# A two-block fp32 transformer on one core: score tiles multiplied apart, tiles moved between engines, SBUF offsets changed

## Chip, cores, metric

The kernel runs on 1 core of one Trainium2 chip. The metric is the time of one execution in device microseconds. The median over several runs counts.

## The reference

Two blocks over 512 tokens of width 1024, all in float32. What the change touches is this (cut):

```python
def gla_chunked(q, k, v, log_f):          # per head: 128 keys, 128 values, chunks of 16 tokens
    ...
    b = jnp.cumsum(log_f, axis=2)
    ...
    q_dec = q * jnp.exp(b)
    k_dec = k * jnp.exp(-b)
    ...

def second_block(x, mem, ...):
    for layer in range(2):
        u = rmsnorm(h, norm_g[layer, 0])
        y = mixer_window_attn(...) if layer == 0 else mixer_hgrn2(...)   # both with cross attention to mem
        h = h + rmsnorm(y, norm_g[layer, 1])
        f = conv_ffn(rmsnorm(h, norm_g[layer, 2]), ...)
        h = h + rmsnorm(f, norm_g[layer, 3])
```

The first block is chunked attention plus a gated convolution and a square-ReLU network of width 4096. The second block has two layers: windowed attention with cross attention, then a gated linear recurrence in both directions (8 heads) with cross attention, each followed by a network of width 2816.

## The kernel before

**Data.** Activations lie feature-major: 8 tiles of 128 features by 512 tokens. Each weight matrix is cut into 128x128 tiles, eight to a slot. SyncE loads 384 slots of 512 KB in a fixed order into a ring of 6 (`w_raw`). GpSimd rounds each slot to a high part `w_hi` and subtracts for a low part `w_lo` (lines 513 to 517; for 40 slots of the recurrence layer ScalarE rounds instead, line 1469). Activations are split the same way. Each weight tile then costs a *triple* on TensorE, three 512-column products on fp32r (`three_passes`, lines 556 to 558): high by high, low activation by high weight, high activation by low weight. The first name in a row such as `acc<-h_hi,w_hi` is the operand that streams, the second the one that is loaded into the array.

**Stages.** `STAGES` (line 61) lists them in the order in which TensorE runs them: six projections of q, k and v, `conv`, `gate`, `proj`, `out`, `up0`, `down0`, `up1`, `down1`, then `a_in`, `memkv`, `a_out`, `ffn_in0`, `ffn_out0`, `b_in`, `b_out`, `ffn_in1`, `ffn_out1`. A stage has column blocks, each of `kt` weight tiles, that add up in one bank of PSUM. A stage in `LEAD` runs its first four column blocks side by side, feature tile by feature tile. `WIDE` (line 59) names stages whose next blocks use banks that are otherwise the attention's (4 and 5 are `ps_s`, 6 is `ps_o`), so that these blocks need not wait until VectorE has taken block 0 (`bank_free`, line 562). `a_out` is not in it.

**Order.** Each engine's instructions are written out by hand in one block per engine, with semaphores between them. There are three attentions. The tiles of projections are interleaved with an attention's units by the table `also`: one unit is scores, maximum, exponential (ScalarE), normalisation (VectorE), transposes (TensorE, `turn`), copy of the transposes to SBUF (ScalarE, `take`, line 1205) and the product with the values (`weigh`, line 727). In the second attention the leading blocks of `a_out` run feature tile by feature tile as soon as each is there (`out_lead`, line 948). The last feature tile is there when ScalarE has copied the last head and VectorE has split it.

**Third attention and recurrence.** While the third attention runs (16 units, from about 1655 to 1696 us), ScalarE also does the first recurrence head's activations: `head_gates(0)` (Silu) after unit 5, `head_sigmoids(0)` after unit 9, `head_forget(0)` after unit 10, `head_logs(0)` after unit 12 (line 1480). Exponential, Silu, Sigmoid and Ln each want a function table of their own. Then come the heads, h = 0 to 7. VectorE keeps the masked scores of a head in `hg_s_f` and `hg_s_b`, computes the states between blocks (`head_states`, line 2061), and adds the two score tiles into `hg_ke_f` (line 2075). TensorE's `head_out` (line 1063) multiplies that sum, and the states, with the values: 4 + 3 + 3 products of 128 columns in full fp32. Each stands as two rows, "x20" for a head. Head h's `head_out` stands in the order of head h+1.

**End.** After the last products VectorE scales each of 8 output tiles and adds it to the residual (`add_norm`, lines 1594 and 1605); SyncE stores them in four pieces of two tiles.

**SBUF.** All offsets are written out (lines 200 to 300). The first tensor starts at byte 16512 of each partition, which is 128 past a multiple of 512. `w_lo`, `w_hi`, `x_res`, `h_hi` and `h_lo` have that same remainder. After the constants come 27 small tensors in steps of 32 bytes, and then a shared part: `rope`, `ffn_tmp`, `rstd_in` and the arena of 96 KB, which holds `qk`, `o_hi`, `o_lo`, `y_hi`, `u_hi`, `u_lo`, `x0_hi`, `hid_hi`, `hid_lo` and the rest by stages. It starts at byte 124608, which is 192 past a multiple of 512 (64 past a multiple of 128). The tensors named here lie multiples of 2048 further on. In `up0` and `up1` feature tile 0 comes from the arena (`x_hi`, `x_lo`) and tiles 1 to 7 from `h_hi` and `h_lo`.

## Time and profile before

| what | value |
|---|---|
| median of 3 runs | 2439.69 us (2438.66 to 2440.32) |
| the profiled execution, own time | 2437.65 us |
| its span, first to last instruction | 2435.9 us |
| TensorE busy | 98% of the span |
| GpSimd, VectorE, ScalarE busy | 60%, 51%, 27% |
| mean granted TensorE clock | 0.993 |

Busy time of TensorE counts each matmul from its start to its end, and these overlap. Its speed is better read from the distance between the starts of two rows. The clock stands at two levels. A share of 1.00 in a window is the full 2.4 GHz, and 0.5 is 1.2 GHz. A number in square brackets behind a row of the timeline is the engine's idle time before it, with the instruction that ended it.

### The profile page before, as it was taken

Reading aid. Unit: us, or ns where it says so; the run is one execution under the profiler, and the core shown is the slowest. Engines: PE = TensorE matmul, PEld = TensorE weight load, DVE = VectorE, ACT = ScalarE, POOL = GpSimd, SP = SyncE. Lnnn points to the kernel's source line nnn. Section 1 sums busy time; section 2 is a strip of 40 time slices with the busy share of each in tenths; the row PEclk is TensorE's granted clock in tenths of the full one; section 3 lists DMA queues with packets and bytes.
Section 4 is the critical chain, followed back from the end, with each engine's and each line's share of the span. In section 5 each row is a group of like instructions: output and inputs, shape, how many; then the busy total and the mean of one; then the engine's idle time right before and its main releaser. Section 6 shows DMA issues by size and latency. Waiting matters only on the chain.

```text
span 2435.9 us, 32669 instructions
## 1 busy us (share of the span) xinstructions
PE 2378.2 (98%) x12126; PEld 1961.1 (81%) x12126; DVE 1231.5 (51%) x2000; ACT 659.7 (27%) x1331; POOL 1466.4 (60%) x1461
## 2 busy tenths in 40 slices
PE   8999999999999999999999999999999999999997
PEld 6877778887888888787788888887888877888885
DVE  4335654334302315777348553044888885755402
ACT  3233321002201213455221110025567643111100
POOL 8654546667666677654458777662344455877761
PEclk9999999999999999999999999999999999999998
DMA  4222222222232322221122222221222212222221
GB/s 169 93 96 87 79 78 97 99 98 88 96 98 98 124 95 87 78 79 62 61 87 96 96 95 95 95 87 53 70 70 70 71 60 78 96 95 97 101 97 52
DMA packets 59762, 214.49 MB, mean 88 GB/s; under 512 B 6624, under 2 KB 6752, under 8 KB 59488
## 3 DMA queue, kind: packets, MB, share of 16 engines
q1 hardware_dynamic: 56880, 206.55, 25.1%
q10 hardware_dynamic: 2736, 5.96, 0.7%
q8 instruction: 97, 1.59, 0.3%
q14 instruction: 49, 0.40, 0.1%
HBM read 210.38 MB, written 2.10 MB: 87 GB/s over the span
## 4 chain that ended last, share of the span: by engine, by line
PE 92%; DVE 5%; ACT 2%; issue 1%; DMA 0%; POOL 0%; DVEq 0%; ACTq 0%; POOLq 0%
PE acc L556 25%; PE acc L558 25%; PE acc L557 24%; PE ps_o L727 2%; PE ps_s L699 2%; PE ps_t L713 2%; PE acc L768 1%; PE acc L770 1%; PE acc L769 1%; PE ps_s L1016 1%; DVE ps_s L1594 1%; PE ps_o L1075 0%; PE ps_s L770 0%; PE ps_s L768 0%; PE ps_s L769 0%
## 5 line engine op out<-in xcount | busy, mean ns | idle before, releaser
L513 POOL CAST w_hi<-w_raw 128x512 fp32r<-128x512 f32 x688 | 439.5, 667 | 709.8 <-DMA w_raw<-stream 709.8
L556 PE MATMUL acc<-h_hi,w_hi 128*128 128x512 f32 (+1 forms) x1844 | 726.0, 394 | 5.5 <-DVE h_lo L1560 2.6
L558 PE MATMUL acc<-h_hi,w_lo 128*128 128x512 f32 (+1 forms) x1844 | 706.7, 383 | 0.0
L557 PE MATMUL acc<-h_lo,w_hi 128*128 128x512 f32 (+1 forms) x1844 | 705.4, 383 | 0.0
L515 POOL TENSOR_TENSOR w_lo<-w_raw,w_hi 128x512 fp32r<-128x512 f32 x384 | 521.6, 1358 | 213.3 <-ACT w_hi L1469 213.3
L517 POOL TENSOR_TENSOR w_lo<-w_raw,w_hi 128x512 fp32r<-128x512 f32 x384 | 534.4, 1392 | 0.0
L556 PEld LDWEIGHTS acc<-h_hi,w_hi 128*128 128x128 f32 x1844 | 348.1, 189 | 73.6 <-DVE h_lo L1560 4.4
L558 PEld LDWEIGHTS acc<-h_hi,w_lo 128*128 128x128 f32 x1844 | 347.2, 188 | 69.8
L557 PEld LDWEIGHTS acc<-h_lo,w_hi 128*128 128x128 f32 x1844 | 348.0, 189 | 65.4 <-issue 1.9
L1616 DVE COPY y_all<-acc 128x512 f32<-128x512 f32 x31 | 21.4, 692 | 269.9 <-PE acc L558 238.5
L556 PE MATMUL acc<-hid_hi,w_hi 128*128 128x512 f32 x352 | 138.9, 395 | 0.0
L558 PE MATMUL acc<-hid_hi,w_lo 128*128 128x512 f32 x352 | 138.0, 392 | 0.0
L557 PE MATMUL acc<-hid_lo,w_hi 128*128 128x512 f32 x352 | 136.6, 388 | 0.0
L1205 ACT ACTIVATE probs_t<-ps_t 128x256 f32<-128x256 f32 (+3 forms) x160 | 68.2, 426 | 240.6 <-PE ps_t L713 240.0
L1638 DVE TENSOR_TENSOR hid_tmp<-acc,rstd_in 128x512 f32<-128x512 f32 x82 | 56.8, 692 | 133.2 <-PE acc L558 130.8
L556 PE MATMUL acc<-u_hi,w_hi 128*128 128x512 f32 x256 | 100.9, 394 | 0.0
L558 PE MATMUL acc<-u_hi,w_lo 128*128 128x512 f32 x256 | 100.4, 392 | 0.0
L557 PE MATMUL acc<-u_lo,w_hi 128*128 128x512 f32 x256 | 99.4, 388 | 0.0
L557 PE MATMUL acc<-o_lo,w_hi 128*128 128x512 f32 x244 | 95.4, 391 | 0.0
L1188 ACT ACTIVATE probs<-probs,neg_max 128x256 f32<-128x256 f32 (+3 forms) x160 | 87.3, 546 | 22.6 <-DVE neg_max L1673 22.4
L1333 ACT ACTIVATE ffn_tmp<-ffn_tmp 128x512 f32<-128x512 f32 x44 | 27.9, 634 | 237.9 <-DVE ffn_tmp L1914 237.9
L1896 DVE TENSOR_TENSOR x_res<-acc,x_res 128x512 f32<-128x512 f32 x16 | 11.1, 692 | 142.8 <-PE acc L558 142.8
(344 smaller groups left out, 3691.0 us busy)
## 6 DMA issues: line engine op xcount, KB each, us to landing
w_raw<-stream SPq DMA_DIRECT2D x384, 512.0 KB, 3.2
toeplitz<-ext_in ACTq DMA_DIRECT2D x16, 256.0 KB, 3.7
out<-x_res SPq DMA_DIRECT2D x4, 512.0 KB, 2.6
x_res<-x_in SPq DMA_DIRECT2D x3, 512.0 KB, 6.8
mem<-mem_in ACTq DMA_DIRECT2D x1, 1024.0 KB, 7.7
consts<-consts_in SPq DMA_DIRECT2D x1, 656.0 KB, 9.3
x_res<-x_in SPq DMA_DIRECT2D x2, 256.0 KB, 5.0
rope<-rope_in ACTq DMA_DIRECT2D x1, 512.0 KB, 9.2
```

Source lines behind the costliest of these rows:

```text
L513: nc.gpsimd.tensor_copy(hi[:, half], raw[:, half]).then_inc(hi_made, 1)
L515: nc.gpsimd.tensor_tensor(lo[:, 0:D // 2], raw[:, 0:D // 2], f32(hi[:, 0:D // 2]), ALU.subtract).then_inc(low_half, 1)
L517: nc.gpsimd.tensor_tensor(lo[:, D // 2:], raw[:, D // 2:], f32(hi[:, D // 2:]), ALU.subtract).then_inc(split_made, 1)
L556: nc.tensor.matmul(ps, hi, x_hi[:, k, 0:cols], start=(k == 0), stop=False)
L557: nc.tensor.matmul(ps, hi, x_lo[:, k, 0:cols], start=False, stop=False)
L558: mm = nc.tensor.matmul(ps, lo, x_hi[:, k, 0:cols], start=False, stop=(k == st.kt - 1))
L699: mm = nc.tensor.matmul(ps_s[i][:, cols], u.q, u.k[:, cols], start=True, stop=True)
L713: mm = nc.tensor.transpose(ps_t[:, b * P:(b + 1) * P], src[:, b * P:(b + 1) * P], const("ident"))
L727: mm = nc.tensor.matmul(ps_o[u.out_part:u.out_part + rows, u.out_cols[0]:u.out_cols[1]], u.v[b], p_t[:, (u0 + 2 * j + i) % 2, b * P:(b + 1 ...
L1188: nc.scalar.activation(p[:, b, 0:u.width], p[:, b, 0:u.width], ACT.Exp, scale=-1.0, bias=small["neg_max"][:, b:b + 1], accum_out=small["ro ...
L1205: nc.scalar.activation(p_t[:, b, 0:u.width], ps_t[:, 0:u.width], ACT.Copy).then_inc(pt_ready, 1)
L1638: step(nc.vector.tensor_tensor(dst, src, by, ALU.mult), st.free)
```

## The change

- `a_out` gets a fifth bank in `WIDE`. Column block 4 uses `ps_s` 0, and its first four tiles run ahead of the last `out_lead`.
- In the third attention ScalarE does the sigmoids, `head_forget(0)` and the logarithms after units 11, 12 and 14, and `head_gates(0)` after the attention.
- VectorE's sum of the two score tiles goes. `head_out` multiplies `hg_s_f` and `hg_s_b` apart, and `hg_chain` is raised by the last state.
- At the end GpSimd handles output tiles 5 and 6: times the gain, times the scale, plus the residual. For that TensorE spreads the scale a second time into `ps_t`, and ScalarE copies it to `rstd_in`. VectorE handles tiles 0 to 4 and 7. The stores are cut 2, 2, 1, 2, 1.
- Six one-column tensors share one place of 32 bytes, and the shared part starts at a multiple of 512 from the first tensor. It now lies at byte 124544, again 128 past a multiple of 512. No other tensor of those named above moves.

```diff
--- before.py
+++ after.py
@@ -56,7 +56,7 @@
 
 
 TOKENS = ["q0", "q1", "k0", "k1", "v0", "v1"]
-WIDE = {"ffn_in0": (4, 5, 6), "ffn_in1": (4, 5, 6), "b_in": (6, 5), "b_out": (4,)}
+WIDE = {"ffn_in0": (4, 5, 6), "ffn_in1": (4, 5, 6), "a_out": (4,), "b_in": (6, 5), "b_out": (4,)}
 LEAD = {*TOKENS, "up0", "memkv", "a_in", "a_out", "ffn_in0", "b_in", "b_out", "ffn_in1"}
 STAGES = [
     *[(name, BANKS, 8) for name in TOKENS], ("conv", 24, 8), ("gate", 16, 8), ("proj", 16, 8), ("out", 8, 8),
@@ -211,15 +211,16 @@
         params = sb("params", [PARAM_W], at)
         at += -(-4 * PARAM_W // 32) * 32
         small = {}
-        for name, n in [("zero", 1), ("k_g8", 1), ("half_gate_b", 16), ("lower", 16), ("one_less", 16), ("less_one", 16), ("eps_d", 1), ("eps_q", 1),
-                        ("eps_v", 1), ("neg_sink", 16), ("neg_max", P_BUFS), ("row_sum", P_BUFS), ("sink_exp", P_BUFS), ("inv_sum", P_BUFS),
+        for name, n in [("half_gate_b", 16), ("lower", 16), ("one_less", 16), ("less_one", 16), ("neg_sink", 16), ("neg_max", P_BUFS), ("row_sum", P_BUFS), ("sink_exp", P_BUFS), ("inv_sum", P_BUFS),
                         ("rms_tok", BLOCKS), ("rstd_tok", BLOCKS), ("eps_tok", BLOCKS),
                         ("head_sums", 16), ("head_root", 16), ("head_inv", 16), ("decay_f", CHUNKS), ("decay_b", CHUNKS),
                         ("block_f", BLOCKS), ("block_b", BLOCKS),
-                        ("lb_exp", 32), ("root_warm", 1), ("rstd_mem", MEM)]:
+                        ("lb_exp", 32), ("columns", 6), ("rstd_mem", MEM)]:
             small[name] = sb(name, [n], at)
             at += -(-4 * n // 32) * 32
-        at = (at + 63) // 64 * 64
+        for i, name in enumerate(["zero", "k_g8", "eps_d", "eps_q", "eps_v", "root_warm"]):
+            small[name] = small["columns"][:, i:i + 1]
+        at = (at + 511) // 512 * 512
         rope = sb("rope", [2, T], at)
         ffn_tmp = sb("ffn_tmp", [2, T], at)
         at += 4 * KB
@@ -379,6 +380,10 @@
         pv_done = sem("pv_done")
         o_taken = sem("o_taken")
         o_copied = sem("o_copied")
+        y_rstd_spare = sem("y_rstd_spare")
+        rstd_copied = sem("rstd_copied")
+        pool_own = sem("pool_own")
+        x_pool = sem("x_pool")
         eps_made = sem("eps_made")
         o_hi_made = sem("o_hi_made")
         gate_ready = sem("gate_ready")
@@ -469,6 +474,7 @@
             st = stages[TOKENS[g]]
             return (tok_made, (BLOCKS - 1) * g + b + 1) if b < BLOCKS - 1 else (slot_done, st.first_slot + st.slots)
 
+        POOL_TILES = (5, 6)
         ACT_SLOTS = range(stages["b_in"].first_slot + 11, stages["b_out"].first_slot + 7)
         block = ctx.enter_context(nc.Block())
 
@@ -490,10 +496,17 @@
                     sp.dma_start(w_raw[:, s, :], stream[bass.ds(it * RING + s, 1)].rearrange("a p n -> p (a n)"))\
                         .then_inc(loaded[s], 16)
 
-            for i in range(0, DT, 2):
-                sp.wait_ge(x_ready, 3 * DT + i + 2)
-                sp.dma_start(out[:, i:i + 2, :], x_res[:, i:i + 2, :]).then_inc(stored, 16)
-            sp.wait_ge(stored, 16 * DT // 2)
+            def store(first, end):
+                sp.dma_start(out[:, first:end, :], x_res[:, first:end, :]).then_inc(stored, 16)
+
+            for first, end in ((0, 2), (2, 4), (4, 5)):
+                sp.wait_ge(x_ready, 3 * DT + end)
+                store(first, end)
+            sp.wait_ge(x_pool, len(POOL_TILES))
+            store(5, 7)
+            sp.wait_ge(x_ready, 3 * DT + DT - len(POOL_TILES))
+            store(7, 8)
+            sp.wait_ge(stored, 16 * 5)
 
 
         @block.gpsimd
@@ -520,6 +533,17 @@
             pool.wait_ge(zero_made, 1)
             for slot in range(n_slots):
                 split(slot)
+            for i in POOL_TILES:
+                y, g = y_all[:, i, :], param("norm_g", 56 + i)
+                pool.wait_ge(y_sq, 3 * DT + i + 1)
+                nc.gpsimd.tensor_tensor(y, y, g.to_broadcast([P, T]), ALU.mult).then_inc(pool_own, 1)
+            pool.wait_ge(rstd_copied, 1)
+            for i in POOL_TILES:
+                y = y_all[:, i, :]
+                pool.wait_ge(pool_own, 2 + (i - POOL_TILES[0]))
+                nc.gpsimd.tensor_tensor(y, y, rstd_in[:], ALU.mult).then_inc(pool_own, 1)
+                pool.wait_ge(pool_own, 3 + (i - POOL_TILES[0]))
+                nc.gpsimd.tensor_tensor(x_res[:, i, :], x_res[:, i, :], y, ALU.add).then_inc(x_pool, 1)
 
         def lagged(cbs, first, upto):
 
@@ -566,7 +590,7 @@
                     pe.wait_ge(before.free, i + 1)
                 elif st.name == "conv":
                     pe.wait_ge(stages["v1"].free, c + 1)
-                elif c == BANKS and st.name != "b_out":
+                elif c == BANKS and st.name not in ("a_out", "b_out"):
                     pe.wait_ge(s_used, n["unit"])
                     out_free()
 
@@ -868,6 +892,11 @@
                 mm.then_inc(y_rstd, 1)
                 if then is not None:
                     turning(then, 9)
+                else:
+                    for b in range(BLOCKS):
+                        mm = nc.tensor.matmul(ps_t[:, b * P:(b + 1) * P], rstd[:, b:b + 1].to_broadcast([P, P]), const("ident"),
+                                              start=True, stop=True)
+                    mm.then_inc(y_rstd_spare, 1)
                 n["o"] += 1
 
             def conv_mlp(layer):
@@ -955,9 +984,13 @@
 
             attention(units_win + units_x[0], probs2, probs2_t, also)
             st = out_st
+            pe.wait_ge(s_used, n["unit"])
+            lead_tiles = BANKS * st.kt
+            block_tiles(st, lead_tiles, lead_tiles + 4, o_hi2, o_lo2)
             for k in range(len(A_OUT_TURNS), st.kt):
                 out_lead(k)
-            mixer_out(st, o_hi2, stages["ffn_in0"])
+            block_tiles(st, lead_tiles + 4, lead_tiles + st.kt, o_hi2, o_lo2)
+            mixer_out(st, o_hi2, stages["ffn_in0"], BANKS + 1)
             conv_mlp(0)
 
             st = stages["b_in"]
@@ -1066,7 +1099,7 @@
                 out_free()
                 for b in range(BLOCKS):
                     cols = slice(b * P, (b + 1) * P)
-                    parts = [(hg_v[:, b, :], hg_ke_f[:, b, :])]
+                    parts = [(hg_v[:, b, :], hg_s_f[:, b, :]), (hg_v[:, b, :], hg_s_b[:, b, :])]
                     if b:
                         parts.append((hg_state_f[:, b - 1, :], hg_qb_f[:, cols]))
                     if b < BLOCKS - 1:
@@ -1476,8 +1509,9 @@
                     nc.scalar.activation(o_hi3[:, X_HEADS + i, 0:T], o2[:, X_HEADS + i, :], ACT.Copy).then_inc(o_hi_made, 1)
 
             act.wait_ge(forget_made, 1)
-            attention(units_x[1], probs2, probs2_t, {5: lambda: head_gates(0), 9: lambda: head_sigmoids(0),
-                                                     10: lambda: head_forget(0), 12: lambda: head_logs(0)})
+            attention(units_x[1], probs2, probs2_t, {len(units_x[1]) - 5: lambda: head_sigmoids(0), len(units_x[1]) - 4: lambda: head_forget(0),
+                                                     len(units_x[1]) - 2: lambda: head_logs(0)})
+            head_gates(0)
             for h in range(HG_HEADS):
                 if h:
                     head_logs(h)
@@ -1522,6 +1556,8 @@
             next_input(lambda i: param("norm_g", 48 + i))
             gelus(1)
             post_norm(stages["ffn_out1"], sq=ffn_tmp)
+            act.wait_ge(y_rstd_spare, 1)
+            nc.scalar.activation(rstd_in[:], ps_t[:], ACT.Copy).then_inc(rstd_copied, 1)
 
 
         @block.vector
@@ -1600,11 +1636,12 @@
                         x_rest(i, next_gain)
 
                 scaled_y(0)
-                for i in range(DT):
+                tiles = [i for i in range(DT) if next_gain is not None or i not in POOL_TILES]
+                for i, after in zip(tiles, tiles[1:] + [None]):
                     step.wait()
                     step(nc.vector.tensor_tensor(x_res[:, i, :], ps_s[i % 2][:], x_res[:, i, :], ALU.add), x_ready)
-                    if i < DT - 1:
-                        scaled_y(i + 1)
+                    if after is not None:
+                        scaled_y(after)
                     rest(i)
                 if next_gain is not None and summed:
                     x_sums()
@@ -2064,15 +2101,14 @@
                     for i in range(BLOCKS - 1):
 
                         b = BLOCKS - 2 - i if d else i
+                        done = hg_chain if d and i == BLOCKS - 2 else None
                         step.wait()
                         if i == 0:
-                            step(nc.vector.tensor_copy(state[:, b, :], u_[:, b, :]))
+                            step(nc.vector.tensor_copy(state[:, b, :], u_[:, b, :]), done)
                         else:
                             over = b + d
                             step(nc.vector.scalar_tensor_tensor(state[:, b, :], state[:, b + 2 * d - 1, :], blk[:, over:over + 1],
-                                                                u_[:, b, :], ALU.mult, ALU.add))
-                step.wait()
-                step(nc.vector.tensor_tensor(hg_ke_f[:], hg_s_f[:], hg_s_b[:], ALU.add), hg_chain)
+                                                                u_[:, b, :], ALU.mult, ALU.add), done)
 
             def head_sums(h):
```

The rows below are the program's instructions in the order of their engine. TensorE at the end of the second attention, before (`mem_v_116` holds its values):

```order
L727 MATMUL ps_o<-probs_t,mem_v_116 128x128 x4
L556 MATMUL acc<-o_hi_120,w_hi 128x512
L557 MATMUL acc<-o_lo_119,w_hi 128x512
L558 MATMUL acc<-o_hi_120,w_lo 128x512
L556 MATMUL acc<-o_hi_120,w_hi 128x512
```

and with the change:

```order
L751 MATMUL ps_o<-probs_t,mem_v_111 128x128 x4
L580 MATMUL ps_s<-o_hi_115,w_hi 128x512
L581 MATMUL ps_s<-o_lo_114,w_hi 128x512
L582 MATMUL ps_s<-o_hi_115,w_lo 128x512
L580 MATMUL ps_s<-o_hi_115,w_hi 128x512
```

After the last `weigh` stood the four triples of the last leading step, into `acc`. Now four triples of column block 4, into `ps_s`, stand ahead of them.

ScalarE in the third attention, from the copy of unit 9 on, before (`probs` rows are the exponentials, 1397 sigmoids, 1450 `head_forget`, 1415 logarithms):

```order
L1205 ACTIVATE probs_t<-ps_t 128x256
L1188 ACTIVATE probs_128,row_sum<-probs_128,neg_max 128x256
L1397 ACT_TABLE_LOAD
L1397 ACTIVATE hg_in_135<-hg_in_135 128x512 x2
L1205 ACTIVATE probs_t<-ps_t 128x256
L1188 ACT_TABLE_LOAD
L1188 ACTIVATE probs_128,row_sum<-probs_128,neg_max 128x256
L1450 ACTIVATE hg_key_f<-hg_in_135,one_less,less_one 128x512
L1450 ACTIVATE hg_key_b<-hg_in_135,one_less,less_one 128x512
L1205 ACTIVATE probs_t<-ps_t 128x256
```

and with the change, from the copy of unit 11 on:

```order
L1238 ACTIVATE probs_t<-ps_t 128x256
L1221 ACTIVATE probs_123,row_sum<-probs_123,neg_max 128x256
L1430 ACT_TABLE_LOAD
L1430 ACTIVATE hg_in_130<-hg_in_130 128x512 x2
L1238 ACTIVATE probs_t<-ps_t 128x256
L1260 ACTIVATE o_113<-ps_o 128x512
L1483 ACTIVATE hg_key_f<-hg_in_130,one_less,less_one 128x512
L1483 ACTIVATE hg_key_b<-hg_in_130,one_less,less_one 128x512
L1238 ACTIVATE probs_t<-ps_t 128x256 x2
L1448 ACT_TABLE_LOAD
L1448 ACTIVATE hg_in_130<-hg_in_130,lower,one_less 128x512 x2
L1238 ACTIVATE probs_t<-ps_t 128x256
```

The last exponential now stands ahead of the first foreign function, so the table of Exp is not loaded again in between. The Silu of `head_gates(0)` stands behind the attention.

TensorE's `head_out`, the first of its four blocks and half of the second, before:

```order
L1075 MATMUL ps_o<-hg_ke_f,hg_v 128x128
L1075 MATMUL ps_o<-hg_qb_b,hg_state_b 128x128
L1075 MATMUL ps_o<-hg_ke_f,hg_v 128x128
L1075 MATMUL ps_o<-hg_qb_f,hg_state_f 128x128
L1075 MATMUL ps_o<-hg_qb_b,hg_state_b 128x128
```

and with the change:

```order
L1108 MATMUL ps_o<-hg_s_f,hg_v 128x128
L1108 MATMUL ps_o<-hg_s_b,hg_v 128x128
L1108 MATMUL ps_o<-hg_qb_b,hg_state_b 128x128
L1108 MATMUL ps_o<-hg_s_f,hg_v 128x128
L1108 MATMUL ps_o<-hg_s_b,hg_v 128x128
```

Each of the four blocks of a head has one product more.

## Rows read from the trace of the kernel before

**Rows 1.** the page, part 1: busy time, share of the span, instructions

```profile
PE 2378.2 (98%) x12126; PEld 1961.1 (81%) x12126; DVE 1231.5 (51%) x2000; ACT 659.7 (27%) x1331; POOL 1466.4 (60%) x1461
```

**Rows 2.** timeline of PE in ffn_in0: start us, us, instruction

```profile
1299.95 0.39 PE L556 MATMUL acc<-h_hi,w_hi 128*128 128x512 f32 x1
...
1310.83 0.39 PE L556 MATMUL acc<-h_hi,w_hi 128*128 128x512 f32 x1
```

**Rows 3.** timeline of PE in ffn_out1, 48 products from row to row

```profile
2299.82 0.39 PE L556 MATMUL acc<-hid_hi,w_hi 128*128 128x512 f32 x1
...
2310.81 0.39 PE L556 MATMUL acc<-hid_hi,w_hi 128*128 128x512 f32 x1
```

**Rows 4.** timeline of PE in up0, 24 products from row to row

```profile
612.91 0.40 PE L556 MATMUL acc<-x_hi,w_hi 128*128 128x512 f32 x1
...
618.42 0.40 PE L556 MATMUL acc<-x_hi,w_hi 128*128 128x512 f32 x1
```

**Rows 5.** groups by line (names, shapes xcount | busy us, mean ns)

```profile
L556 PE MATMUL acc<-hid_hi,w_hi 128*128 128x512 f32 x352 | 138.9, 395 | 0.0
L556 PE MATMUL acc<-u_hi,w_hi 128*128 128x512 f32 x256 | 100.9, 394 | 0.0
L557 PE MATMUL acc<-o_lo,w_hi 128*128 128x512 f32 x244 | 95.4, 391 | 0.0
L556 PE MATMUL acc<-y_hi,w_hi 128*128 128x512 f32 x64 | 25.2, 394 | 0.0
```

**Rows 6.** timeline of PE, end of the second attention [idle before <-releaser]

```profile
1200.17 1.05 PE L727 MATMUL ps_o<-probs_t,mem_v 128*128 128x128 f32 x8
1203.09 0.50 PE L556 MATMUL acc<-o_hi,w_hi 128*128 128x512 f32 x1 [1.87 <-DVE o_lo L1538]
...
1206.91 0.50 PE L556 MATMUL acc<-o_hi,w_hi 128*128 128x512 f32 x1 [0.78 <-DVE y_all L1616]
```

**Rows 7.** timeline of ACT in the third attention

```profile
1671.60 1.28 ACT L1188 ACT_TABLE_LOAD   x1
...
1678.72 1.15 ACT L1397 ACTIVATE hg_in<-hg_in 128x512 f32<-128x512 f32 x2
...
1681.96 0.80 ACT L1450 ACTIVATE hg_key_f<-hg_in,one_less,less_one 128x512 f32<-128x512 f32 x1
...
1688.57 1.52 ACT L1415 ACTIVATE hg_in<-hg_in,lower,one_less 128x512 f32<-128x512 f32 x2
```

**Rows 8.** timeline of PE in the same attention

```profile
1683.87 2.05 PE L727 MATMUL ps_o<-probs_t,mem_v 128*128 128x128 f32 x8 [2.55 <-ACT probs_t L1205]
...
1690.50 2.02 PE L727 MATMUL ps_o<-probs_t,mem_v 128*128 128x128 f32 x8 [2.12 <-ACT probs_t L1205]
...
1694.94 0.35 PE L727 MATMUL ps_o<-probs_t,mem_v 128*128 128x128 f32 x1
```

**Rows 9.** windows: us, PE, PEld, DVE, ACT, POOL busy (x), PEclk, DMA

```profile
1680.00:1694.00 14.00, 9.14 (x37) 7.58 (x38) 3.23 (x5) 8.52 (x16) 0.00 (x0) 0.76 0.00 0
```

**Rows 10.** chain of waits, head stage: start us, us, engine, line

```profile
1819.73 2.23 PE ps_o L1075 x20
```

**Rows 11.** waits of PE: us in total, times, longest

```profile
PE ps_s L1016 <- DVE hg_s_f L2167: 2.4, 1, 2.4
PE ps_s L1016 <- DVE hg_block_k L2132: 2.1, 1, 2.1
PE ps_t L1041 <- ACT ffn_tmp L1427: 1.4, 1, 1.4
```

**Rows 12.** groups by line, DVE

```profile
L2075 DVE TENSOR_TENSOR hg_ke_f<-hg_s_f,hg_s_b 128x512 f32<-128x512 f32 x8 | 10.2, 1272 | 0.3
```

**Rows 13.** timeline of DVE at the end of the program

```profile
2420.72 0.76 DVE L1594 SCALAR_TENSOR_TENSOR ps_s<-y_all,params,ps_o 128x512 f32<-128x512 f32 x1 [1.31 <-PE ps_o L866]
...
2432.13 0.69 DVE L1605 TENSOR_TENSOR x_res<-ps_s,x_res 128x512 f32<-128x512 f32 x1
```

**Rows 14.** the page, part 5: GpSimd

```profile
L515 POOL TENSOR_TENSOR w_lo<-w_raw,w_hi 128x512 fp32r<-128x512 f32 x384 | 521.6, 1358 | 213.3 <-ACT w_hi L1469 213.3
```

## The prediction, made before any run of the changed kernel

> **What bounds the kernel.** I read the page first, then TensorE's rows in order of time, then its waits, then the other engines only where TensorE waits for them. TensorE is busy for 98% of the span [rows 1], so time comes from three places: the pace of its products, the few places where it waits, and the tail after its last product. Anything else is hidden under it.
>
> The pace is not the same everywhere. In `ffn_in0`, where `h_hi` and `h_lo` stream, 48 products take 10.88 us, 226.7 ns each [rows 2]. In `ffn_out1`, where `hid_hi` and `hid_lo` stream from the shared part of SBUF, the same 48 products take 10.99 us, 229.0 ns each [rows 3]. The instruction, its size and its weights are of the same kind in both, and the operands differ in where they lie: 128 past a multiple of 512 against 192 past. In `up0` one triple in eight comes from the shared part, and 24 products take 5.51 us where the pace of rows 2 would give 5.44 [rows 4]. So the triple from the shared part also slows its neighbours, or itself more than in rows 3.
>
> **The change, part by part.** The sum is made against the profiled execution, 2437.65 us. It is 2.04 us under the median of 2439.69, so I add the sum to the median for the number asked.
>
> *A, the fifth bank of `a_out`.* The last `weigh` starts at 1200.17 and issues eight passes. Its follower could start at 1201.06 (eight passes at 2.23 / 20 = 0.11 us each [rows 10]). It waits 1.87 us for VectorE's split, runs four triples (12 x 0.229 = 2.75 us), then waits 0.78 us for bank 0, and block 4 starts at 1206.91 [rows 6]. Now four triples of block 4 fill the first wait (2.75 us of work against 1.87), and the last leading step follows at once: 24 products from 1201.06 end at 1206.56. Before, the same 24 products would have ended at 1206.91 + 2.75 = 1209.66. **A = -3.1 us.** Blocks 5 to 7 find their banks taken by then. Bounds: 0 if the ring has no slot ready for block 4 (its place came free long before), -3.1 at most.
>
> *B, ScalarE's work in the third attention.* Inside the attention ScalarE now loads five tables, with the change two. A load takes 1.28 us, the Silu about half of the pair of sigmoids' 1.15 us [rows 7]. Out of the attention go the load and Silu (1.9 us) and two loads for Exp (2.6 us), 4.5 us in all. What stays is 2.4 us for the sigmoids, two times 0.80 us for `head_forget`, and 1.28 + 1.52 us for the logarithms. TensorE stands on this chain: it waits 2.55 and 2.12 us for ScalarE's copies before two `weigh` [rows 8]. After both waits its clock is at 1.2 GHz for a time: in the 14 us around them the granted clock is 0.76 [rows 9], and eight passes take 2.05 us instead of 1.13 [rows 8]. **B = -4.5 us**, the work taken off. Waits of 1 to 2 us stay, before units 13 and 15 and the last two `weigh`. Bounds: -2.1 (one wait goes, the other and both slow stretches return) and -8.1 (both waits, 4.7, and 0.24 x 14 = 3.4 us of clock). The Silu moves behind the attention, ahead of head 0's exponentials, but these start earlier by more than the 1.9 us that it costs. I cost this at nothing: the column blocks of head 1 lie between the attention and head 0's first scores, and cover it. If that cover were gone, 1.9 us would come back.
>
> The Trainium skill (page "ScalarE: Activation LUTs", section "What ACT_TABLE_LOAD costs") gives 1.28 us for the load and 1.38 us more of drain for every switch. The row agrees on the first number. By an estimate from the page the three loads fewer would be worth 4.1 us more.
>
> *C, the two score tiles.* A head gains four fp32 products of 128 columns, eight passes. Twenty passes take 2.23 us [rows 10], so a head costs 0.89 us more and the eight heads 7.1 us, on an engine without slack. VectorE loses eight sums of 1.27 us mean [rows 12], 10.2 us, but TensorE waits for VectorE or what hangs on it in three places of the head stage only: 1.4 us once for `head_root`, whose input waits in ScalarE behind VectorE, and 2.1 and 2.4 us in the last head [rows 11]. At the first the sum goes from the path and TensorE arrives 0.89 us later: the wait of 1.4 us closes. In the last head VectorE's chain is shorter by one sum (I take 0.9, a sum without contention) and TensorE's 0.89 us fall into the wait. **C = 7.1 - 1.4 - 1.8 = +3.9 us.** Bounds: +7.1 if no wait closes, and 7.1 - 5.9 = +1.2 if all three do. That VectorE's freed time is worth all its 10.2 us is excluded by the absence of waits in heads 2 to 6.
>
> *D, the end.* VectorE takes 2432.13 - 2420.72 = 11.41 us from its first row to its last, for 15 steps of 0.76 each; two tiles fewer are four steps [rows 13]. That is -3.0 us. GpSimd has finished its slots by then. It multiplies by the gain beforehand, then waits for TensorE's second spread (eight passes, 0.9 us, up to twice that at the low clock) and ScalarE's copy (0.6, as half of the pair in rows 7), and needs four steps of about 1.36 us [rows 14]. From 2420.5, when the first spread is there, this ends between 2427.4 and 2428.5, before VectorE at 2429.8. SyncE's queue has GpSimd's store ahead of the last one, so if GpSimd were late, both would be. The last store is half as large, for which I take 0.2. **D = -3.2 us.** Bounds: +0.5 (GpSimd's steps take twice as long) and -3.8.
>
> *E, the shared part at a multiple of 512.* The triples that stream from it: 352 + 256 + 244 + 64 = 916 [rows 5]. If these take rows 2's pace, a triple saves (10.99 - 10.88) / 16 = 6.9 ns, 6.3 us in all. In `up0` and `up1` 28 column blocks save 0.07 us each [rows 4], 2.0 us. **E = -8.3 us.** Bounds: 0, and +12 (below). I take the full value because rows 4 speak against the distance into SBUF as the cause: there the neighbours in `h_hi` are slow as well, so the change from one alignment to the other plays a part, and the change makes all of them alike.
>
> The rule that speaks against this: the Trainium skill (page "SBUF — State Buffer", section "Specifications (TRN2)") gives lines of 16 bytes. Both 124608 and 124544 are multiples of 16, so by it E is 0 and the time is that of the first rival.
>
> **Sum:** -3.1 - 4.5 + 3.9 - 3.2 - 8.3 = -15.2 us. That is 2422.5 us for an execution like the profiled one, and **2424.5 us** against the median.
>
> **Rivals.**
> 1. *The alignment does nothing.* The cause of rows 3 against rows 2 is something else, for instance how deep in SBUF the operands lie. For it: rows 3 and rows 2 are also different stages and regions. Against it: rows 4. E = 0: 2439.69 - 6.9 = 2432.8 us. Chance 0.2.
> 2. *Equal alignment collides (slower).* Weights and streamed operand then start at the same remainder in every triple, and each triple of the shared part costs what `x_hi` costs in rows 4: 5.51 us less 21 products of 226.7 ns is 0.75 us, if its neighbours are not slow, against 0.687 us in rows 3; with the neighbours' share out I take 0.70 us. Then 916 x 0.013 = +12 us, and the time is 2439.69 - 6.9 + 12 = 2444.8 us. It decides from 6.9 / 916 = 7.5 ns per triple on. Against it: in rows 2 weights and operand have the same remainder already and are the fastest. Chance 0.04.
> 3. *The products are paid in full, and the waits of the third attention move instead of going.* B = -2.1, C = +7.1: 2439.69 - 9.6 = 2430.1 us. For it: the logarithms still stand between two copies, and one wait of about 2 us was enough for the low clock. Chance 0.12.
>
> **Numbers.** The forecast case has 0.64; its own range is 2420.5 to 2428.5 by the bounds of B and C. The range that should hold 8 in 10 reaches to rivals 1 and 3: 2419.5 to 2433.5. About 0.2% (4.9 us) is what a measurement of this kernel can tell from no change. Faster needs under 2434.8: the forecast, rival 3 and nearly all of rival 1, 0.91. Rivals 1 and 3 together give 2438.4, and a weak rival 2 lies there too: 0.05 within. Slower: 0.04.
>
> **What would show it.** E: 48 products of `ffn_out1` in 10.88 us, and 24 in `up0` in 5.44. A: no idle time of TensorE between the last `weigh` of the second attention and block 5. B: last `weigh` of the third attention starting about 4.5 us earlier after A and E are taken off, and a clock above 0.76 there. C: 28 passes in `head_out`, 3.1 us, the wait on `head_root` gone, the waits of the last head shorter by about 1.8 us together. D: VectorE's last row 9 us after its first, GpSimd's last before it. The prediction is wrong if rows 3's pace stays, if heads 2 to 6 do not grow by 0.89 us each, or if the last store waits for GpSimd.

## The result, and the profile after

The changed kernel takes 2425.11 us (median of 4 runs, 2423.87 to 2426.22), the kernel before 2439.18 us in the same comparison. The ratio is 0.9942, with a 95% interval of 0.9924 to 0.9959. That is 14.1 us faster. The prediction was 2424.5 us.

The profiled execution took 2426.22 us, with a span of 2423.5 us. TensorE is as busy as before [rows 1], with 72 instructions more. The page, part 1:

```profile
PE 2374.2 (98%) x12198; PEld 1965.9 (81%) x12198; DVE 1224.9 (51%) x1988; ACT 659.5 (27%) x1330; POOL 1471.2 (61%) x1467
```

**The pace (term E).** The timeline of TensorE in `ffn_out1`, 48 products from row to row (start us, us, instruction), and then 24 products in `up0`:

```profile
2291.01 0.39 PE L580 MATMUL acc<-hid_hi,w_hi 128*128 128x512 f32 x1
...
2301.89 0.39 PE L580 MATMUL acc<-hid_hi,w_hi 128*128 128x512 f32 x1
```

```profile
612.61 0.39 PE L580 MATMUL acc<-x_hi,w_hi 128*128 128x512 f32 x1
...
618.05 0.39 PE L580 MATMUL acc<-x_hi,w_hi 128*128 128x512 f32 x1
```

The 48 products take 10.88 us, the pace of rows 2, where rows 3 had 10.99. The 24 take 5.44 us, where rows 4 had 5.51.

**The end of the second attention (term A).** The timeline of TensorE:

```profile
1196.56 1.05 PE L751 MATMUL ps_o<-probs_t,mem_v 128*128 128x128 f32 x8
1197.37 0.48 PE L580 MATMUL ps_s<-o_hi,w_hi 128*128 128x512 f32 x1
...
1200.19 0.39 PE L580 MATMUL acc<-o_hi,w_hi 128*128 128x512 f32 x1
...
1202.91 0.39 PE L580 MATMUL ps_s<-o_hi,w_hi 128*128 128x512 f32 x1
```

Rows 6 showed 1.87 us of idle time, four triples, 0.78 us of idle time, and block 4. Now four triples of block 4 (`ps_s`) start 0.81 us after the last `weigh`, the last leading step (`acc`) follows, and then the rest of block 4. No wait is left.

**The third attention (term B).** The timelines of TensorE and of ScalarE [in brackets the idle time before, and what ended it], and TensorE's window around them:

```profile
1674.36 0.44 PE L737 MATMUL ps_t<-consts,probs 128*128 128x128 f32 x2 [1.09 <-ACT probs_t L1238]
...
1676.62 1.13 PE L751 MATMUL ps_o<-probs_t,mem_v 128*128 128x128 f32 x8 [1.12 <-ACT probs_t L1238]
...
1681.63 1.13 PE L751 MATMUL ps_o<-probs_t,mem_v 128*128 128x128 f32 x8 [2.04 <-ACT probs_t L1238]
```

```profile
1671.59 1.28 ACT L1430 ACT_TABLE_LOAD   x1
...
1672.88 1.15 ACT L1430 ACTIVATE hg_in<-hg_in 128x512 f32<-128x512 f32 x2
...
1678.40 1.28 ACT L1448 ACT_TABLE_LOAD   x1
1679.70 1.52 ACT L1448 ACTIVATE hg_in<-hg_in,lower,one_less 128x512 f32<-128x512 f32 x2
1681.12 0.36 ACT L1238 ACTIVATE probs_t<-ps_t 128x256 f32<-128x256 f32 x1
```

```profile
1671.00:1686.00 15.00, 10.75 (x61) 8.34 (x60) 5.24 (x11) 12.07 (x21) 0.00 (x0) 1.00 0.11 36
```

Three waits stand here, of 1.09, 1.12 and 2.04 us, where rows 8 had 2.55 and 2.12. The last one ends at ScalarE's copy of 1681.12, which stood behind the table load and the logarithms. In this execution the clock stayed at full speed (1.00, where rows 9 had 0.76). That was not so in the others, as the experiments show.

**The heads (term C).** The chain of waits, one head's `head_out`, and TensorE's waits on VectorE in the last head (us in total, times, longest):

```profile
1806.79 3.12 PE ps_o L1108 x28
```

```profile
PE ps_s L1049 <- DVE hg_s_f L2203: 3.3, 1, 3.3
PE ps_s L1049 <- DVE hg_block_k L2168: 0.8, 1, 0.8
```

The 28 passes take 3.12 us instead of 2.23 for 20 [rows 10]. The wait for `head_root` is gone. In the last head the two waits are now 0.8 and 3.3 us. Before they were 2.1 and 2.4 [rows 11], so together they shrank by 0.4 us, not by 1.8. What that means for the stretch is told with the run that undoes the sum.

**The end (term D).** The timelines of VectorE and of GpSimd:

```profile
2411.53 0.76 DVE L1630 SCALAR_TENSOR_TENSOR ps_s<-y_all,params,ps_o 128x512 f32<-128x512 f32 x1 [1.37 <-PE ps_o L890]
...
2419.91 0.69 DVE L1642 TENSOR_TENSOR x_res<-ps_s,x_res 128x512 f32<-128x512 f32 x1
```

```profile
2413.91 1.27 POOL L544 TENSOR_TENSOR y_all<-y_all,rstd_in 128x512 f32<-128x512 f32 x1 [15.44 <-ACT rstd_in L1560]
...
2417.82 1.27 POOL L546 TENSOR_TENSOR x_res<-x_res,y_all 128x512 f32<-128x512 f32 x1
```

VectorE's last row starts 8.38 us after its first, where rows 13 had 11.41. GpSimd's last step starts at 2417.82, and takes 1.27 us, so it is done before VectorE.

**The span, cut at marks.** Single runs of one kernel scatter by several us here, but the trace can be cut at marks on TensorE. Each entry below is worked out from the start times of two rows. The marks are: the last product of the second attention's last `weigh` (I ends), the first product of `ffn_out0` (II ends), the start of the last row of products with the keys of head 0 (III), the same of head 6 (IV), the last product of head 7's `head_out` (V), the last product of `ffn_out1` (VI), the end of the span (VII). "Again" is the changed kernel run a second time (told below as "The changed kernel again").

| kernel | I | II | III | IV | V | VI | VII |
|---|---|---|---|---|---|---|---|
| before | 1200.9 | 288.1 | 246.2 | 227.5 | 45.0 | 409.0 | 19.1 |
| changed | 1197.3 | 284.4 | 240.1 | 231.4 | 46.8 | 407.5 | 15.9 |
| changed, again | 1195.8 | 284.6 | 241.8 | 231.4 | 47.0 | 407.4 | 15.9 |
| E undone (64 apart) | 1201.0 | 284.7 | 242.1 | 231.6 | 45.7 | 409.1 | 15.9 |
| shared part 128 apart | 1204.8 | 285.3 | 244.3 | 231.2 | 44.8 | 411.4 | 15.9 |
| B undone | 1196.3 | 284.5 | 245.0 | 231.4 | 47.0 | 407.4 | 15.9 |
| C undone | 1195.1 | 284.5 | 241.9 | 227.4 | 45.9 | 407.4 | 15.9 |
| D undone | 1196.2 | 284.6 | 241.5 | 231.4 | 45.5 | 407.4 | 19.1 |
| A undone | 1196.2 | 287.7 | 240.8 | 231.4 | 45.7 | 407.4 | 16.1 |
| before, E alone | 1196.6 | 287.8 | 242.6 | 227.3 | 46.9 | 407.4 | 19.1 |

Read downwards, each edit shows in its own columns: A in II, B in III, C in IV and V, D in VII, E in I, III and VI. Stretches II, IV, VI and VII mostly repeat within 0.2 us where an edit doesn't touch them. I, III and V do not. Among the kernels of the table with the new offsets, I takes 1195.1 to 1197.3 us (a wait of 1.2 us for `v_feat` in the first profile is a part of that), III takes 240.1 to 241.9 with ScalarE's new order, and V takes 45.5 to 47.0.

### The profile page after: what moved, and what is told of

It is laid out like the page before. It is cut to its first block, busy times and chain, and to the rows that moved or that the text cites. A ratio compares the mean times of both kernels' runs of the same rounds, so it can differ in the third digit from the quotient of the medians.

```text
span 2423.5 us, 32808 instructions
## 1 busy us (share of the span) xinstructions
PE 2374.2 (98%) x12198; PEld 1965.9 (81%) x12198; DVE 1224.9 (51%) x1988; ACT 659.5 (27%) x1330; POOL 1471.2 (61%) x1467
## 4 chain that ended last, share of the span: by engine, by line
PE 93%; DVE 5%; ACT 1%; issue 1%; DMA 0%; POOL 0%; DVEq 0%; POOLq 0%
PE acc L580 25%; PE acc L582 24%; PE acc L581 24%; PE ps_s L723 3%; PE ps_o L751 2%; PE ps_t L737 2%; PE acc L792 1%; PE acc L794 1%; PE acc L793 1%; PE ps_o L1108 1%; PE ps_s L1049 1%; PE ps_s L1038 1%; PE ps_s L581 1%; PE ps_s L582 1%; PE ps_s L580 1%
```

## The experiments

The interval of a ratio below is about 0.0014 to either side, 3.4 us, unless another is given. The runs were made in three groups. The kernel before had medians of 2438.78, 2438.07 and 2438.35 us in them, so medians of different groups can be set side by side to within about 1 us. The expectations were written before each run.

### The alignment undone

```diff
         at = (at + 511) // 512 * 512
+        at += 64
```

> The changed kernel with the shared part 64 bytes further on, at byte 124608 as before; everything else as changed. Theory (where an operand starts sets the pace): the 48 products of ffn_out1 take 10.99 us again instead of 10.88, and the time is 8 us over the changed kernel, 2433 us (about 0.9967 of the kernel before). Rival (the faster pace comes from something else in the change, for instance that the order of the work shifted): the pace stays at 10.88 us and the time within 2 us of 2425.

Measured: 2432.42 us, ratio 0.9971 (0.9960 to 0.9982), 7.3 us over the first median of the changed kernel and 7.4 over the second. The timeline of TensorE in `ffn_out1`, 48 products:

```profile
2299.94 0.39 PE L581 MATMUL acc<-hid_hi,w_hi 128*128 128x512 f32 x1
...
2310.93 0.39 PE L581 MATMUL acc<-hid_hi,w_hi 128*128 128x512 f32 x1
```

They take 10.99 us again. The theory holds, the rival falls: 64 bytes decide the pace, and nothing else in the change.

### 128 bytes further on

```diff
+        at += 128
```

> The changed kernel with the shared part 128 bytes further on, at byte 124672: a multiple of 128 but 256 past a multiple of 512, while h_hi, h_lo and the weights stay at 128 past. Theory 1 (a multiple of 128 is enough): ffn_out1's 48 products in 10.88 us, up0's 24 in 5.44, time within 1.5 us of the changed kernel, 2425. Theory 2 (the remainder of 512 has to agree with that of the weights or of h_hi): 10.99 us or more, and 2433 us. Theory 3 (only the triples beside h_hi mind the remainder of 512): ffn_out1 in 10.88 us, up0 in 5.51, 2427 us.

Measured: 2440.79 us, ratio 1.0013 (1.0004 to 1.0022), slower than the kernel before.

```profile
2305.52 0.39 PE L581 MATMUL acc<-hid_hi,w_hi 128*128 128x512 f32 x1
...
2316.72 0.39 PE L581 MATMUL acc<-hid_hi,w_hi 128*128 128x512 f32 x1
```

The 48 products take 11.20 us, 700 ns a triple against 680 in the changed kernel. Being a multiple of 128 is not enough, and theories 1 and 3 fall. Theory 2 had the right side, but its 2433 us were 8 us short: 128 bytes off cost three times as much as 64. Over 916 triples, 20 ns each would be 18 us; 15.7 were measured.

`up0` shows that the distance of a triple's own operands is not all. A column block there has one triple from the shared part (`x_hi`, `x_lo`) and seven from `h_hi` and `h_lo`, which never leave distance 0. At 64 bytes the eight triples take 703, 698, 691, 697, 684, 680, 680 and 680 ns (each the median of 26 blocks, in the run before this one), and at 128 bytes 696, 694, 690 and then 680. So the triples behind a misplaced one are slow as well, and here 128 bytes cost less than 64.

### All of SBUF 128 bytes further on

```diff
-        base = (nc.sbuf_base + 63) // 64 * 64
+        base = (nc.sbuf_base + 63) // 64 * 64 + 128
```

> The changed kernel with every tensor of SBUF 128 bytes further on: weights, h_hi, h_lo and the shared part all start 256 past a multiple of 512. The shared part alone at 256 had cost 15 us (700 ns a triple instead of 680). Theory (only the distance between the streamed operand and the weights, modulo 512, counts): triples stay at 680 ns everywhere and the time within 2 us of the changed kernel, 2425. Rival (the absolute remainder counts, 128 is good and 256 is bad): the triples from h_hi and h_lo take about 700 ns too, and with some 1,790 of them beside the 916 the time is 35 us over the shared-part-alone case, about 2475 us.

Measured: 2424.52 us, ratio 0.9941, beside 2425.03 for the changed kernel in the same group.

```profile
2289.86 0.39 PE L580 MATMUL acc<-hid_hi,w_hi 128*128 128x512 f32 x1
...
2300.74 0.39 PE L580 MATMUL acc<-hid_hi,w_hi 128*128 128x512 f32 x1
```

10.88 us. The shared part starts where it did in the run before, 256 past a multiple of 512, and there is no loss, since the weights have moved with it. So the remainder itself doesn't count, and a distance does. It is taken for the distance to the weights because, beside what streams, only `w_hi` and `w_lo` are read by these products. No run moved the weights alone.

### 256 bytes further on

```diff
+        at += 256
```

> The changed kernel with the shared part 256 bytes further on: streamed operand and weights then start 256 apart modulo 512 (0 apart in the changed kernel: 680 ns a triple; 64 apart: 687; 128 apart: 700). Theory 1 (the cost grows with the distance): 700 ns a triple or more, 2441 us or more. Theory 2 (the pattern repeats every 256 bytes): 680 ns and 2425 us.

Measured: 2423.86 us, ratio 0.9946.

```profile
2290.51 0.39 PE L581 MATMUL acc<-hid_hi,w_hi 128*128 128x512 f32 x1
...
2301.39 0.39 PE L581 MATMUL acc<-hid_hi,w_hi 128*128 128x512 f32 x1
```

10.88 us again. Theory 2 holds: a distance of 256 is as good as none, 64 costs 6.9 ns a triple, 128 costs 20. Other distances were not tried, and why the distance matters is not shown. This run also puts the shared part deeper in SBUF than any other, at no loss.

### The kernel before with the new offsets alone

The list of small tensors and the rounding to 512 are taken over, nothing else.

> The kernel before with the new offsets alone (six one-column tensors in one place, shared part at byte 124544); order of the work, products and tail as before. Theory (the alignment acts by itself): ffn_out1's 48 products in 10.88 us, and 7.4 us faster than the kernel before, as its undoing in the changed kernel had cost, 2431 us. Rival (part of the gain hangs on the other edits, because faster products only arrive earlier at waits set by ScalarE and VectorE): 4 to 5 us faster only, 2434 us, with longer waits in the second and third attention.

Measured: 2429.86 us, ratio 0.9969 (0.9959 to 0.9978), 8.5 us faster than the kernel before (2438.35). The 48 products of `ffn_out1`:

```profile
2290.07 0.39 PE L557 MATMUL acc<-hid_hi,w_hi 128*128 128x512 f32 x1
...
2300.95 0.39 PE L557 MATMUL acc<-hid_hi,w_hi 128*128 128x512 f32 x1
```

They take 10.88 us, and the theory holds. Not all of the gain is pace, though. Stretch III is 3.6 us shorter than in the kernel before. 1.0 us of that lies ahead of the third attention, and 2.6 us in and behind it, with ScalarE's order still the old one. The rows are shown with the next run. Stretch V is 1.9 us longer.

### ScalarE's work in the third attention back in its places

```diff
-            attention(units_x[1], ..., {len(units_x[1]) - 5: ..., len(units_x[1]) - 4: ..., len(units_x[1]) - 2: ...})
-            head_gates(0)
+            attention(units_x[1], ..., {5: lambda: head_gates(0), 9: lambda: head_sigmoids(0),
+                                        10: lambda: head_forget(0), 12: lambda: head_logs(0)})
```

> The changed kernel with ScalarE's work of the first recurrence head back at its old places (Silu after unit 5, sigmoids after 9, forget after 10, logarithms after 12). Theory (term B): the waits of about 2.5 and 2.1 us before two weighs and the half clock behind them return, 4.5 us slower, 2429.5 us. Rival (B was nothing: the waits were set by something else and moved with the alignment): within 1 us of 2425, waits of the third attention of the same sum.

Measured: 2426.86 us, ratio 0.9952. That is 1.8 us over the second run of the changed kernel, and the fastest runs of the two are 3.2 us apart (2425.76 and 2422.54). Stretch III is longer by 3.1 us (245.0 against 241.8 in that second run). The timeline of TensorE, and the windows of this kernel and of the changed one, again:

```profile
1671.00 0.44 PE L737 MATMUL ps_t<-consts,probs 128*128 128x128 f32 x2 [0.61 <-ACT probs_t L1238]
...
1674.68 1.94 PE L751 MATMUL ps_o<-probs_t,mem_v 128*128 128x128 f32 x8 [2.54 <-ACT probs_t L1238]
...
1681.20 1.65 PE L751 MATMUL ps_o<-probs_t,mem_v 128*128 128x128 f32 x8 [1.94 <-ACT probs_t L1238]
```

```profile
1670.00:1688.00 18.00, 12.91 (x58) 10.34 (x57) 4.96 (x11) 10.99 (x22) 0.03 (x1) 0.81 0.05 15
```

```profile
1671.00:1686.00 15.00, 10.75 (x51) 8.16 (x50) 4.59 (x9) 12.07 (x19) 1.30 (x2) 0.89 0.11 35
```

TensorE idles 5.4 us in this attention, all waits added up, and 4.25 in the changed kernel. So in this pair 4.5 us of ScalarE's work are worth 1.2 us of waits. The rest is the clock: 0.81 over these 18 us, where `weigh` takes 1.94 us instead of 1.13. In the changed kernel it is 0.89 over 15 us in the second profile and 1.00 in the first, and stretch III was 1.7 us shorter in the first.

The kernel before with the new offsets alone has the old order too, and loses less by it. Two rows of TensorE there:

```profile
1678.27 1.13 PE L728 MATMUL ps_o<-probs_t,mem_v 128*128 128x128 f32 x8 [2.55 <-ACT probs_t L1206]
...
1683.96 1.13 PE L728 MATMUL ps_o<-probs_t,mem_v 128*128 128x128 f32 x8 [1.16 <-ACT probs_t L1206]
```

The second wait is 1.16 us instead of 1.94, and both `weigh` run at full clock (0.91 over 1670 to 1688). From the first `weigh` of the third attention to the end of stretch III the old order takes 72.3, 72.1 and 69.8 us (before, this run, offsets alone), and the new order 67.3 to 69.0 in all eleven profiles that have it. The new order is faster in every pair, by 0.8 us at the least, 5.0 at the most and 2.9 between the two averages. So the theory had the mechanism right. Its size was too large in this pair and on average, and depends on what the clock does behind the waits.

### The sum of the score tiles back in all heads

```diff
+                    if True:
+                        parts = [(hg_v[:, b, :], hg_ke_f[:, b, :])]
...
+                if True:
+                    step.wait()
+                    step(nc.vector.tensor_tensor(hg_ke_f[:], hg_s_f[:], hg_s_b[:], ALU.add), hg_chain)
```

> The changed kernel with VectorE's sum of the two score tiles back for all eight heads, and one product tile per block instead of two. Theory (term C, the products cost more on TensorE than the sum): heads 1 to 6 are 0.89 us shorter each, the wait for head_root of 1.4 us is back and the last head waits about 1 to 2 us more; in all 3.9 us faster than the changed kernel, 2421.2 us. Rival (the freed time of VectorE is worth more than the products): the kernel gets slower than 2425, because waits for VectorE return in more than two places.

Measured: 2419.87 us (2419.04 to 2422.10), ratio 0.9924 (0.9910 to 0.9938). This is 5.2 us under the changed kernel, and no other run of the study is faster by more than noise. TensorE's waits:

```profile
PE ps_s L1049 <- DVE hg_block_k L2173: 2.4, 1, 2.4
PE ps_s L1049 <- DVE hg_s_f L2208: 2.1, 1, 2.1
PE ps_t L1074 <- ACT ffn_tmp L1462: 1.4, 1, 1.4
```

Heads 1 to 6 are 0.89 us shorter each, and the wait for `head_root` is back: stretch IV is 4.0 us shorter, as the theory says. The theory stands, and the rival falls.

In the last head VectorE sets the time, and this can be measured at its own marks. From the last product with the keys of head 6 to VectorE's first mask of head 7 it is 26.7 to 26.8 us in the five executions whose head 6 has the sum, and 26.05 in eight of the nine with products (25.9 in the ninth). From there to its last mask it is 9.9 us with the sum (four executions in the same order), and 9.4 to 9.6 without. VectorE's chain is shorter by 0.7 and by 0.3 to 0.6 us, and TensorE's 0.89 us of head 6 vanish in the waits. The sizes of the two waits hide this. In the kernel before the score products between them ran partly at half clock (eight of them took 1.92 us), which used up a part of the second wait: it is 2.39 us there, and 2.81 in the kernel before with the new offsets, where the same eight took 1.50. Behind the last mask the products of head 7 and the clock come in. Stretch V as a whole shows no difference that stands out from the clock: 44.8 to 47.0 us in nine executions with products, and 45.0, 45.9 and 46.9 in three with the sum.

### The changed kernel again

> The changed kernel itself once more, beside the others of this group, as their yardstick. Expected 2425 us, ratio to the kernel before 0.994. If it comes out near 2424 or near 2426 in single runs, that is the scatter seen at first (two runs at 2424.0, two at 2426.2), and the place of the 2 us should show in the trace as the wait for v_feat in a_in (1.2 us, at 990.7) with or without a slow clock behind it.

Measured: 2425.03 us (2422.54 to 2426.76), ratio 0.9942 (0.9928 to 0.9955). The result repeats. The guess on the scatter falls: the wait for `v_feat` was 1.2 us in the first profile (2426.22 us) and 0.2 in this one, which was no faster (2426.76 us). Here 1.7 us of slow clock in stretch III took its place.

The last head scatters too. TensorE's window in it, in this profile and in that of the run with all of SBUF 128 bytes further on, where the waits are the same 0.8 and 3.3 us:

```profile
1980.00:1993.00 13.00, 9.59 (x47) 8.62 (x48) 11.28 (x14) 0.60 (x1) 11.50 (x11) 0.74 0.01 2
```

```profile
1980.00:1993.00 13.00, 8.64 (x60) 7.70 (x60) 11.97 (x14) 0.60 (x1) 11.96 (x11) 1.00 0.06 15
```

With the clock at 0.74 stretch V takes 47.0 us, with 1.00 it takes 44.9. The same waits are followed by low clock in one execution and not in another, and this is worth 2 us.

### The end as before

The code of GpSimd, the second spread, ScalarE's copy and the five stores are taken out, and the four stores put back.

> The changed kernel with the end as before: VectorE scales and adds all eight output tiles, four stores of two tiles. Theory (term D): the stretch from TensorE's last row in ffn_out1 to the end of the span is 16.3 us again instead of 13.2, 3.2 us slower, 2428.3 us. Rival (the last store waits for SyncE's queue or the bus, not for VectorE): under 1 us slower.

Measured: 2427.17 us, ratio 0.9956, 2.1 us over the changed kernel. Stretch VII is 19.1 us against 15.9: 3.2 us, as expected. (The expectation counts from the row that spreads the scale, 2.8 us behind this mark.) The run gains about 1.5 us of it back in stretch V, by the clock. The rival falls.

### `a_out` without the fifth bank

```diff
-WIDE = {..., "a_out": (4,), ...}
...
-            pe.wait_ge(s_used, n["unit"])
-            lead_tiles = BANKS * st.kt
-            block_tiles(st, lead_tiles, lead_tiles + 4, o_hi2, o_lo2)
             for k in range(len(A_OUT_TURNS), st.kt):
                 out_lead(k)
-            block_tiles(st, lead_tiles + 4, lead_tiles + st.kt, o_hi2, o_lo2)
-            mixer_out(st, o_hi2, stages["ffn_in0"], BANKS + 1)
+            mixer_out(st, o_hi2, stages["ffn_in0"])
```

> The changed kernel without the fifth bank of a_out (its column blocks 4 to 7 all after the last leading step, as before). Theory (term A): the waits of 1.9 and 0.8 us around block 4 return and it is 3.1 us slower, 2428.1 us; from the comparison of the stretches in the first traces I now expect 2.8 us. Rival (the waits had been shifted to VectorE's next step anyway): under 1 us slower.

Measured: 2428.17 us, 3.1 us over the changed kernel. The ratio is 0.9964, which beside the changed kernel's 0.9942 would be 5.4 us; the interval is 3.4 us to either side, and the stretch decides. The timeline of TensorE:

```profile
1198.31 0.50 PE L580 MATMUL acc<-o_hi,w_hi 128*128 128x512 f32 x1 [1.88 <-DVE o_lo L1570]
...
1202.10 0.50 PE L580 MATMUL acc<-o_hi,w_hi 128*128 128x512 f32 x1 [0.78 <-DVE y_all L1649]
```

Both waits of rows 6 are back, within a hundredth, and stretch II is 3.2 us longer. The theory holds.

### The sum in heads 1 to 7, and the block decays later in the last head

```diff
+                    if h:
+                        parts = [(hg_v[:, b, :], hg_ke_f[:, b, :])]
...
-                if h:
+                if 0 < h < HG_HEADS - 1:
                     head_blocks(h)
...
                 if h == HG_HEADS - 1:
                     split_out(X_HEADS + h - 1, o_hi3)
+                    head_blocks(h)
```

> The changed kernel with VectorE's sum back for heads 1 to 7 and two products only in head 0 (whose sum costs a wait of 1.35 us for head_root), and in the last head the products by block decays (head_blocks) moved behind the scores' masks, so that they no longer stand between TensorE's score tiles 0 and 2. Theory 1 (the wait of 2.05 us before level 2 is the place of head_blocks on VectorE): this wait is under 0.5 us, 0.5 us from head 0, 1.2 us in the last head, 1.7 us faster than with all sums, 2418.2 us. Theory 2 (VectorE is busy without a break there, so the wait only moves to the last head_out): 0.5 us from head 0 alone, 2419.4 us, and a wait of about 2.5 us before the last head_out.

Measured: 2423.98 us (2419.65 to 2425.24), ratio 0.9938, 4 us slower than with all sums. TensorE's waits:

```profile
PE ps_o L1110 <- DVE hg_ke_f L2116: 4.4, 1, 4.4
PE ps_s L1049 <- DVE hg_block_k L2173: 2.4, 1, 2.4
PE acc L580 <- DVE o_lo L1576: 2.3, 2, 1.6
```

The wait before level 2 is gone and came back larger: 4.4 us before the last `head_out`, with 1.6 us more before a leading step (the longest of the third row). Stretch V takes 49.0 us instead of 45.9, `head_out` itself running at half clock. Theory 2 named the mechanism. Neither expected the loss. The 0.5 us of head 0 came (from the keys of head 0 to those of head 1 it is 38.7 us instead of 39.2), but a wait of 0.54 us for `head_root` appears further on, at 1854.1 us.

### A leading step moved into the wait

The sum is back in all heads, and in the last head:

```diff
                 head_in(h + 1, 4)
+                if h == HG_HEADS - 1:
+                    out_lead(9)
                 head_scores(h, 2)
...
-            out_lead(9)
```

> The changed kernel with VectorE's sum back in all heads, as in the fourth run, and in the last head the leading step of feature tile 9 of b_out put ahead of the last two score products, into the wait for VectorE. Theory 1 (the wait is 2.05 us long and the 2.75 us of work fill it; VectorE's states can then start 0.8 us sooner): the wait before level 2 is gone, a wait of 1 to 1.5 us before the products with the keys takes its place, 1 us faster than the fourth run, 2418.9 us, ratio 0.992. Theory 2 (VectorE's chain alone sets this stretch): within 0.5 us of the fourth run.

Measured: 2420.90 us (2417.97 to 2421.34), ratio 0.9925, not to be told from the version with all sums (2419.87). TensorE's waits:

```profile
PE ps_s L1049 <- DVE hg_block_k L2174: 2.4, 1, 2.4
PE ps_s L1085 <- issue: 1.7, 1, 1.7
PE acc L580 <- DVE o_lo L1577: 1.7, 2, 1.0
PE ps_s L1049 <- DVE hg_s_f L2209: 0.9, 1, 0.9
PE ps_o L1110 <- DVE hg_ke_f L2117: 0.5, 1, 0.5
```

"The fourth run" in the expectation is the version with all sums. One wait of 2.1 us became four: 1.7, 1.0 (the longest of the third row), 0.9 and 0.5. Stretch V takes 45.8 us against 45.9. By the stretch theory 2 holds: work moved on TensorE doesn't shorten it, and VectorE's chain is left as what sets it. The median is 1.0 us over the version with all sums, and not within 0.5. In the profiles the end is longer by 0.9 us (16.8 against 15.9), because the spread of the scale ran at half clock there and took 2.04 us instead of 1.13.

## Why the prediction was right

The forecast case came true in its mechanisms, and one of its five sizes, B, was too large by most of the measurements.

**E, forecast -8.3: right.** Undone it costs 7.4 us beside the second run of the changed kernel, and alone in the kernel before it brings 8.5. It was read from rows 2 and 3, one instruction at two paces. Rows 4, where the neighbours in `h_hi` looked slow as well, were read rightly too: in the run that undoes E the triples behind the misplaced one take up to 698 ns. Rival 1 (depth in SBUF, another stage) falls, since 64 bytes back bring the slow pace with everything else equal. Its rule was the Trainium skill's (page "SBUF — State Buffer", section "Specifications (TRN2)"), which gives lines of 16 bytes; all four offsets tried are multiples of 16, so by the lines alone they are equal. They took 680, 687, 700 and 680 ns a triple, and the measurement decides. Another rule bears on it: the Trainium skill (page "TensorE: Matmul & The Clock Gate", section "Step-by-step: what each phase is for") says that TensorE reads streamed operand and weights through two independent ports, so that loading the next weights takes nothing from the running product. By that alone the distance between the two would not matter. Here it changes the pace by 1% at 64 bytes and 3% at 128. Rival 2 had a real effect but its sign turned round: equal remainders are a fast case, and 128 apart is the slow one.

**A, forecast -3.1: right.** 3.1 us by the medians, 3.2 us in stretch II.

**D, forecast -3.2: right.** 3.2 us in stretch VII; the order of VectorE and GpSimd at the end as worked out.

**B, forecast -4.5: the step that was too large.** It took the work off ScalarE as the gain on TensorE. Undone in the changed kernel it costs 1.2 us of waits, and clock for the rest: 1.8 us by the medians (under the bound of 2.1), 3.1 in stretch III. Over all pairs of profiles with the old and the new order it is 0.8 to 5.0 us, and 2.9 between the averages. Two reasons can be read in the rows. The logarithms still stand in front of a copy that a `weigh` waits for (2.04 us, before 2.12), and the sigmoids and `head_forget`, now later, make two waits of 1.1 us of their own. And the clock, which I let go with the waits, mostly stays: it was low after the last wait in the second profile. The prediction's estimate of 4.1 us more for three table loads fewer finds nothing in the rows: the load at 1671.59 us starts 0.02 us behind the end of the activation before it, and the next activation starts 1.29 us after that. Nor does the load at 1678.40 leave more than its own length.

**C, forecast +3.9: right in size, with one reading to mend.** Measured +5.2 by the medians, whose interval is 3.4 us to either side. By the trace stretch IV has +4.0, where the working had six heads at 0.89 less 1.4 for `head_root`, +3.9. For the last head it had 0.89 twice less 1.8, that is nothing, and stretch V shows nothing beyond the clock. What failed is the observable: I wrote that the waits of the last head would be shorter by 1.8 us together, and they are by 0.4. A wait is the distance between two engines, and in the kernel before TensorE had come late to the second one, at half clock. With the new offsets alone the two waits are 2.4 and 2.8 us, 1.1 more than in the changed kernel.

From the kernel before to the second profile of the changed one the seven stretches change by -5.1, -3.5, -4.4, +3.9, +2.0, -1.6 and -3.2 us, -12 together. They can be shared out among the terms. E has all of I and VI, 0.3 of II, and the 1.0 us of III that lies ahead of the third attention: -8.0, and no surer than stretch I, which scatters by up to 2.2 us. A has -3.2 in II, B the other -3.4 in III, C +3.9 in IV, D -3.2 in VII. That leaves +2.0 in V, which is not one of the forecast's terms. The granted clock in the last head was 0.74 in this profile; in the runs with all of SBUF moved and with 256 bytes, whose two waits there are the same, stretch V takes 44.9 us.

By the medians the gain is 14.1 us, and 13.0 in the group of that second run, where the forecast was 15.2. The medians of the single undoings add up to 9.2 us (3.1 + 1.8 - 5.2 + 2.1 + 7.4), each with its 3 us of interval. Between executions of one kernel the clock behind the waits moves stretch III by 1.7 us and stretch V by 2. I take that for the rest, without a run that shows it. That the median came out 0.6 us from the forecast is partly luck: in the traces B was 1.1 us too large, the clock in stretch V was not in the sum, and the medians of the kernel before alone lie up to 1.6 us apart from group to group.

Rival 3 (B = -2.1, C = +7.1) was half true: the logarithms stand between two copies as it said, but the wait for `head_root` did go.

## What to carry to other kernels

Where one instruction has two paces in two places of a profile, compare the operands' addresses before anything else. Here 64 bytes between where the streamed operand and the weights start were worth 1% of every product and 128 bytes 3%, and rounding one offset brought more than any move of work. Before work is moved from an engine with slack in places to one without any, count the places where the first is waited for: here there was one such wait up to the last head, of 1.4 us, and the products cost 5.3 us there. And when a wait in a stretch that another engine fills without a break is closed by reordering, look for it further down: twice it came back, once with interest.
